# Seven blocks of eight small fp32 matmuls, results unused, in the TensorE stream of a four-layer hybrid encoder step

## The reference, cut to what matters

```python
for i in range(DEPTH):                                  # 4
    a_p = rms_norm(hp, norm_mix[i]); a_s = rms_norm(hs, norm_mix[i])
    ...                                                 # input projection, mixer, output projection
    hp = hp + o_p
    hs = hs + o_s
    hp = hp + sq_relu_mlp(rms_norm(hp, norm_mlp[i]), mlp_w_up[i], mlp_w_down[i])
    hs = hs + sq_relu_mlp(rms_norm(hs, norm_mlp[i]), mlp_w_up[i], mlp_w_down[i])

def sq_relu_mlp(x, w_up, w_down):                       # w_up 1024 x 4096, w_down 4096 x 1024
    h = jax.nn.relu(x @ w_up)
    return (h * h) @ w_down
```

## Time and profile before

| | us |
|---|---|
| median of 3 runs | 2777.91 |
| the runs | 2777.91, 2768.42, 2779.39 |
| the profiled execution | 2769.5 |
| its span, first to last instruction | 2767.8 |
| PE busy (matmuls) | 2738.1 |
| DVE busy | 1264.1 |
| ACT busy | 857.6 |
| POOL busy | 223.8 |

### The profile page before, as it was taken

The page is one execution under the profiler, slowest core; times in us unless marked ns, Lnnn a source line. Parts: engine busy times, 40 slices in busy tenths (PEclk is TensorE's granted clock), DMA queues, the critical chain, the costliest instruction groups (busy, mean ns, idle before and its releaser), DMA issues.

```text
span 2767.8 us, 48400 instructions
## 1 busy us (share of the span) xinstructions
PE 2738.1 (99%) x20754; PEld 2666.3 (96%) x20754; DVE 1264.1 (46%) x1577; ACT 857.6 (31%) x933; POOL 223.8 (8%) x232
## 2 busy tenths in 40 slices
PE   8999999999999999999999999999999999999998
PEld 8987999999999999999999899999999969999998
DVE  4258534333455434334477643333442494433333
ACT  3147322122311323223233532322321373321222
POOL 4000100000211100000132210000010001000001
PEclk9999999999999999999999999999999999999999
DMA  4210322222222222222221122222232103222221
GB/s 158 77 65 32 116 86 78 90 77 91 76 85 82 77 91 77 91 79 89 77 62 62 54 77 92 76 77 91 76 107 77 46 36 129 89 81 87 78 89 50
DMA packets 205540, 223.64 MB, mean 81 GB/s; under 512 B 3766, under 2 KB 200480, under 8 KB 205392
## 3 DMA queue, kind: packets, MB, share of 16 engines
q1 hardware_dynamic: 200992, 206.06, 23.1%
q0 software_dynamic: 4400, 15.41, 1.6%
HBM read 208.60 MB, written 12.86 MB: 80 GB/s over the span
## 4 chain that ended last, share of the span: by engine, by line
PE 97%; DVE 1%; ACT 1%; issue 0%; DMA 0%; POOL 0%; ACTq 0%; DVEq 0%
PE bank L394 88%; PE bank L499 2%; PE bank L459 1%; PE bank L520 1%; PE bank L691 1%; PE bank L467 0%; PE bank L559 0%; PE bank L639 0%; PE bank L414 0%; PE bank L746 0%; DVE wlo L1182 0%; PE bank L453 0%; DVE e L1287 0%; PE bank L745 0%; PE bank L568 0%
## 5 line engine op out<-in xcount | busy, mean ns | idle before, releaser
L394 PE MATMUL bank<-ahi,whi 128*128 128x288 f32 x3584 | 770.6, 297 | 6.8 <-DVE alo L1207 6.8
L394 PE MATMUL bank<-ahi,wlo 128*128 128x288 f32 x3584 | 766.5, 295 | 0.0
L394 PE MATMUL bank<-alo,whi 128*128 128x288 f32 x3584 | 765.8, 295 | 0.0
L851 ACT ACTIVATE whi<-raw 128x2048 fp32r<-128x2048 f32 x191 | 364.7, 1909 | 835.1 <-PE bank L394 828.3
L394 PEld LDWEIGHTS bank<-ahi,whi 128*128 128x128 f32 x3584 | 577.1, 189 | 11.6 <-DVE wlo L1182 7.0
L394 PEld LDWEIGHTS bank<-ahi,wlo 128*128 128x128 f32 x3584 | 577.0, 189 | 0.0
L394 PEld LDWEIGHTS bank<-alo,whi 128*128 128x128 f32 x3584 | 576.9, 189 | 0.0
L394 PE MATMUL bank<-hhi,whi 128*128 128x288 f32 x2560 | 549.0, 296 | 3.8 <-DVE hlo L1543 2.0
L394 PE MATMUL bank<-hhi,wlo 128*128 128x288 f32 x2560 | 547.0, 295 | 0.0
L394 PE MATMUL bank<-hlo,whi 128*128 128x288 f32 x2560 | 546.5, 295 | 0.0
L1182 DVE TENSOR_TENSOR wlo<-raw,whi 128x2048 fp32r<-128x2048 f32 x192 | 444.1, 2313 | 210.0 <-ACT whi L851 207.7
(11 more groups left out here) (247 smaller groups left out, 1511.9 us busy)
## 6 DMA issues: line engine op xcount, KB each, us to landing
raw<-in_mlp_w_up SPq DMA_DIRECT2D x64, 1024.0 KB, 5.4
raw<-in_mlp_w_down SPq DMA_DIRECT2D x64, 1024.0 KB, 5.1
raw<-in_sb_w_qkv SPq DMA_DIRECT2D x24, 1024.0 KB, 5.3
raw<-in_conv_w_in SPq DMA_DIRECT2D x12, 1024.0 KB, 5.1
raw<-in_gla_w_in SPq DMA_DIRECT2D x12, 1024.0 KB, 5.3
raw<-in_sb_w_o SPq DMA_DIRECT2D x8, 1024.0 KB, 5.2
out<-mixs POOLq DMA_DIRECT2D x2, 2048.0 KB, 7.6
out<-big POOLq DMA_DIRECT2D x2, 2048.0 KB, 8.3
```

Of the source, the lines that this page charges most:

```text
L394: mm = pe.matmul(acc[h][:, 0:HALF], w[:, u, k, m * P:(m + 1) * P], a[:, k, h * HALF:(h + 1) * HALF], start=(k == 0 and w is whi and a is a ...
L851: act.activation(whi[:, 1 - u], raw[:, 1 - u], ACT.Copy).then_inc(w_hi, 1)
```

## The change

A function `interlude` is added to the TensorE program and called in `project` behind the second chunk of the second slab, (s, m) = (1, 1), of every projection with a norm except `norm` = 4, so in the input projections of layers 0, 1 and 3 and in each of the four MLPs. It has four matmuls with the 128x128 identity as weights and 64 columns of the identity (16 out of every 32) into bank 7, and four with 64 columns of it as weights and 32 columns into bank 6 beyond column 384. Nothing reads these places; there is no wait and no semaphore.

```diff
+                        if norm is not None and norm != 4 and isinstance(s, int) and (s, m) == (1, 1):
+                            interlude()
                         if between is not None:
                             between(s, m)
                 slabs(pe, count, body, peel(count, norm, between is not None))
+
+            def interlude():
+                def blocks(w):
+                    return ident[:, 0:w].rearrange("p (b s) -> p b s", s=32)[:, :, 16:32]
+
+                for i in range(4):
+                    pe.matmul(bank[7][:, 64 * i:64 * i + 64], ident[:], blocks(P), start=True, stop=True)
+                for i in range(4):
+                    pe.matmul(bank[6][0:64, 384 + 32 * i:416 + 32 * i], ident[:, 16 * i:16 * i + 64], blocks(64), start=True, stop=True)
```

## The result

The changed kernel took 2792.09 us (median of 9 runs, 2788.9 to 2793.3), the kernel before 2777.91 (9 runs, 2755.59 to 2779.98). The ratio is 1.0065 with a 95% interval of 1.0047 to 1.0082: slower by 0.65% (the two medians alone give 1.0051), where 1.26% faster was forecast. Of the 49 us between forecast and result, 48 lie in one step, as will be seen. The spread tells as much as the median: before has runs from 2755.6 to 2780.0, after only from 2788.9 to 2793.3.

What follows compares the result with a forecast made beforehand. TensorE was taken to bound the kernel, busy without waits in the changed stretches. Profiled 2769.5 us plus 11.6 for the blocks minus 38.1 for the fast pace gave 2743.0 us, -1.26% against the median; range 2738 to 2784.

Steps and rivals of the forecast that it cites:

- The bound: Whole kernel: TensorE is busy 2738.1 of 2767.8 us without waits here, so inserted work costs its own duration.
- Two paces at one clock: Line 394's matmuls: 133.3 or 130.0 ns each at the same clock, each pace holding until the next foreign matmul.
- The cost of the blocks: Seven added blocks in the TensorE stream: 1.66 us each, 11.6 us in all.
- the bounds of 8.2 and 26.9: Limits in us on the seven blocks' cost, with all records as cheap or as dear as other traced ones.
- The estimate of 9.0 us: Seven blocks' cost from weight-load times alone: 1.28 us a block, leaving out breaks between the kinds.
- What it may give back: Behind all seven places: the block, copying layer 2's block ending, selects the fast pace; 38.1 us gained.
- The MLP of layer 1: Gain behind the block in this MLP: 0, since it ran fast in the profiled run anyway.
- (b): Rival: the block gives no fast pace and ends one it finds, in layer 1's MLP; 2790.9 us, chance 0.14.
- (a): Rival: the block doesn't set the pace, entry phase may matter; whole insertion is paid, 2781.1 us, chance 0.14.
- (c): Rival: only some places turn fast; each missing big stretch costs 9.1 to 9.8 us, 2753 to 2772; chance 0.22.
- (d): Rival: the change doesn't do what it says, its unused matmuls being removed; no time or chance of its own.
- The range: Whole kernel: 2738 to 2784 us, taking in the unset-pace case and leaving out the case of ended fast pace.

Runs made afterwards that it cites:

- e11: As e7, plus the same three matmuls again in the third slab in the MLPs of layers 0 and 3; 2740.10 us, ratio 0.9879 to before.
- e3: Probe: kernel before with one of ten kinds of foreign matmuls (one is none) behind nearly every chunk of the four MLPs; 2917.87 us.
- e6: Probe: kernel before with a bf16 matmul, then one of twelve matmul kinds behind k = 4 or 5, in nearly every MLP chunk; 3098.73 us.
- e8: Probe like e6, with operands varied: layer 2's block and others taken from a large tile or from the identity; 3207.27 us.
- e7: Kernel before with, at the seven places, bf16 matmuls behind k = 0 and 4 and one narrow fp32 matmul behind k = 7; 2755.78 us, ratio 0.9941.
- e1: Changed kernel with the block moved ahead of the two sums of squares instead of behind the second slab; 2788.49 us, ratio 1.0041 to before.

## Why the prediction was wrong, point by point

**The bound** was right: PE without a wait, and what is inserted costs its duration. (VectorE is busy 40% of a stretch at the fast pace, 159.81 of 401.00 us, not 39%; nothing hung on it.)

**Two paces at one clock, 3.3 ns apart, each of which holds itself** was right, and so was the reading of before's two levels of time as stretches at one pace or the other. Nine runs of before show more levels than the two that I had seen (2755.6 and 2761.1 too), which I take for more than one stretch at once; these runs left no trace. That both paces hold I had only from the MLPs; e11 shows the fast one in all seven stretches, in two of them through 2928 matmuls.

**The cost of the blocks**, 11.6 us, measured 11.3. The narrow range of the earlier trace rows was worth more than the bounds of 8.2 and 26.9. The estimate of 9.0 us from the Trainium skill ("TensorE: Matmul & The Clock Gate", section on LDWEIGHTS) came out 2.3 us low; the trace has 112 and 58 ns from record to record within the two kinds, where the page's rule gives 107 and 53, and 205 ns at the change from one to the other.

**What it may give back** is the step that failed: "the copy selects the fast pace wherever it stands". It rested on one chunk of 48 matmuls and it was wrong in two ways. The block of layer 2 gives the fast pace only when it is entered third, seven of seven against none of six, so its shape alone is not what selects. The two blocks that rows 5 set side by side, `half` = 16 and `half` = 8, differed in this too: in before's trace the one was entered third, the other first. To read their difference as one of the run length was the slip. And the change's block, though its matmuls have the same shapes, is no copy in the sense that counts. In the changed kernel it was entered third at three places, first at one and at the fast pace at three, and was slow behind all seven. In the probes 4 wide and 4 narrow were never fast at any entry (46 cases with runs of 16 or 8 in e3, more in e6 and e8), nor were 8 and 4. The sum was thus off by the whole -38.1 us.

**The MLP of layer 1** was entered with 0, "fast in the profiled run anyway". That was the second error in the same step: a fast pace that comes by chance at the slab border ahead of the block is ended by the block, at three of three places of the changed kernel and nine of nine in e3. The term was worth +10.0 and not 0 against the profiled execution. That no block ended it in the profiled run of the changed kernel, where it hadn't begun, is chance; with the block behind the border the most that it could have kept is the 0.3 us of two chunks. Over all nine runs the lowest rises by 33 us (2755.6 to 2788.9) and the highest by 13 (2780.0 to 2793.3); 11.3 of each are the blocks, and the rest I take to be the fast stretches that are gone.

**The rivals.** (b) is what happened: the block gives nothing and ends the fast pace that it finds. Its price came out too, 2790.9 worked out and 2792.09 measured, in part by luck, since it took its 9.8 from the MLP of layer 1, where in the profiled run there was nothing to end, and didn't have the 1.5 of the clock. It had 0.14. Rows 5 had the evidence for it, the block at 1447.14 that ended a fast chunk; and the profile had one observation for the gain and one against it. A fair weight would have been nearer to one half. The doubt named under (a), the phase of entry, was well founded: it decides behind layer 2's block and behind one or three narrow matmuls. It isn't the whole cause, since behind the added block every phase is slow. (c) found no case, as no place took. (d) was not the case: the page has 112 records more, two for each of the 56 matmuls. The range, to 2784, left out just the case that came.

**Open.** Why layer 2's block, entered third, is followed by the fast pace and a block of its count is not, from either tile. The last gap ahead of it is 130 ns in layer 2 and 135 with the weights from the identity, but with weights from the large tile it was 130 or 131 too, and slow all the same. What the hidden part of the state is that made the first attempt fail in the MLPs of layers 0 and 3, and what in the first attempt changes it: a bf16 matmul alone doesn't (e7 has two ahead), nor do the two fp32 sums of line 414, which stand ahead of every first attempt. No mechanism inside PE is shown by these runs; the rule found is one of what follows what.

## What to carry to other kernels

Where PE is the bound and one shape repeats thousands of times, divide stretch by count along the chain before anything else: two stretches with the same instructions and another quotient are a finding, and so are run times in levels. A single favourable piece in a trace is a hypothesis, and a probe kernel that repeats each candidate some twenty times in one profile costs one run and can settle it. Work that is put into such a stream must be judged by what it does to the pace behind it and to a pace that it finds, not by its own duration alone: here 11 us of duration came with a loss of 10 between the two profiled runs, and some 6 us of other matmuls (nine times about 0.7) brought, net of their cost, some 39 against the highest runs of before (2780.0) and 33 by the ratio.

## What the runs showed of the hardware that I had not expected

- The same stream of matmuls (128x128 weights, 288 columns, fp32r, a weight load each) runs at 133.3 or at 130.0 ns a matmul at a granted clock of 1.00, and stays in either through 2928 matmuls (390.59 us in the changed kernel's trace, 380.86 in e11).
- After the two fp32 sums of line 414 the fast pace may begin by itself at the next slab border. Counted over all the traces: never (0 of 44) where the sums were entered third, 14 of 38 where they were entered first, 0 of 15 where they were entered at the fast pace, and 2 of 7 where the change's block stood right ahead of them (e1). I take before's spread of 24 us to come from this; only one of its runs left a trace.
- One fp32 matmul with 64 weight columns and 32 columns selects the fast pace in 62 of 62 cases in the probes when the long gap stands first of the last four, and in 0 of 45 when it stands third; three do the same (20 of 20 and 0 of 20), two or four hardly ever do (2 of 28 entered first, 0 of 33 entered third).
- One bf16 matmul of 128 columns costs 0.12 us in this stream (0.13 when it is entered first) and ended the fast pace in all 64 cases of e6 and e8 in which it found it; what it leaves is the slow one in a known rhythm.
